# ScalarE's order in the prompt attention: exponentials of block i ahead of the copies of block i-1

## The reference, cut to what matters

```
s = (q_nope . k_nope + q_pe . k_pe) * SCALE      # 128 queries x (i+1)*128 keys
s = where(causal, s, -1e30)
pr = softmax(s)
out_block = pr @ v
```

## Time and profile before

| | |
|---|---|
| time, median of 3 runs | 2477.78 us (2474.61 to 2484.24) |
| the profiled execution's own time | 2484.98 us |
| its span | 2483.2 us |
| mean granted TensorE clock | 0.959 of full speed |
| busy share of the span | PE 93%, DVE 54%, ACT 25%, POOL 16% |
| the prompt attention's blocks | 1011 to 1315 us of the span, four pairs |

### The profile page before, as it was taken

The page is one execution under the profiler, slowest core; times in us unless marked ns, Lnnn a source line. Parts: engine busy times, 40 slices in busy tenths (PEclk is TensorE's granted clock), DMA queues, the critical chain, the costliest instruction groups (busy, mean ns, idle before and its releaser), DMA issues.

```text
span 2483.2 us, 36895 instructions
## 1 busy us (share of the span) xinstructions
PE 2314.1 (93%) x14466; PEld 2146.1 (86%) x14466; DVE 1351.2 (54%) x2071; ACT 632.7 (25%) x1043; POOL 388.6 (16%) x248
## 2 busy tenths in 40 slices
PE   6999999999998998788877879999999999999896
PEld 6999999999998997455444559999999999999896
DVE  6444444444446642887688973644444444444746
ACT  5211111111113241333332342311111111112523
POOL 0000000000000001999999100000000000000000
PEclk9999999999999999788879989999999999999998
DMA  4111111111111104000013511111111111111201
GB/s 142 49 45 42 42 42 51 34 51 51 51 51 34 51 26 51 14 14 13 0 47 102 163 54 37 51 52 51 42 43 50 37 48 50 35 51 51 67 27 70
DMA packets 53998, 123.01 MB, mean 50 GB/s; under 512 B 9985, under 2 KB 30882, under 8 KB 53730
## 3 DMA queue, kind: packets, MB, share of 16 engines
q1 hardware_dynamic: 47730, 112.92, 15.4%
q10 hardware_dynamic: 5264, 5.67, 0.8%
q0 software_dynamic: 928, 3.38, 0.4%
HBM read 115.85 MB, written 6.09 MB: 49 GB/s over the span
## 4 chain that ended last, share of the span: by engine, by line
PE 79%; DVE 11%; ACT 4%; issue 3%; DMA 1%; SPq 1%; ACTq 0%; DVEq 0%
PE ps L426 24%; PE ps L428 23%; PE ps L427 23%; PE ps L587 4%; DVE cacc L1593 2%; PE ps L612 1%; PE ps L602 1%; ACT pr L1047 1%; DVE cacc L1511 1%; DVE cacc L1509 1%; PE ps L744 1%; DMA raw<-in_wstream 1%; DVE rstd L1209 1%; DVE q L1527 1%; ACT sq L810 1%
## 5 line engine op out<-in xcount | busy, mean ns | idle before, releaser
L426 PE MATMUL ps<-n_hi,wlo 128*128 128x352 f32 x2832 | 924.6, 326 | 27.2 <-DVE wlo L1192 11.7
L428 PE MATMUL ps<-n_hi,whi 128*128 128x352 f32 x2832 | 914.4, 323 | 0.0
L427 PE MATMUL ps<-n_lo,whi 128*128 128x352 f32 x2832 | 913.1, 322 | 0.0
L426 PEld LDWEIGHTS ps<-n_hi,wlo 128*128 128x128 f32 x2832 | 535.5, 189 | 31.3 <-DVE wlo L1192 12.6
L427 PEld LDWEIGHTS ps<-n_lo,whi 128*128 128x128 f32 x2832 | 537.0, 190 | 2.1 <-issue 0.2
L428 PEld LDWEIGHTS ps<-n_hi,whi 128*128 128x128 f32 x2832 | 536.1, 189 | 0.0
L1257 DVE TENSOR_TENSOR gu<-ps,rstd 128x704 f32<-128x704 f32 x132 | 117.6, 891 | 506.8 <-PE ps L428 506.8
L426 PE MATMUL ps<-hid_hi,wlo 128*128 128x352 f32 x1104 | 360.9, 327 | 18.5 <-DVE h L1239 18.3
L428 PE MATMUL ps<-hid_hi,whi 128*128 128x352 f32 x1104 | 356.7, 323 | 0.0
L427 PE MATMUL ps<-hid_lo,whi 128*128 128x352 f32 x1104 | 356.2, 323 | 0.0
L1239 DVE SCALAR_TENSOR_TENSOR h<-ps,h 128x352 f32<-128x352 f32 x552 | 273.7, 520 | 150.4 <-PE ps L428 149.2
(11 more groups left out here) (181 smaller groups left out, 1854.4 us busy)
## 6 DMA issues: line engine op xcount, KB each, us to landing
raw<-in_wstream SPq DMA_DIRECT2D x167, 512.0 KB, 3.6
ctile<-in_cache SPq DMA_DIRECT2D x100, 144.0 KB, 2.4
ctile<-in_cache ACTq DMA_DIRECT2D x28, 144.0 KB, 2.7
pw<-in_pairw SPq DMA_DIRECT2D x4, 800.0 KB, 4.4
h<-in_xT SPq DMA_DIRECT2D x2, 1408.0 KB, 9.8
out_yT<-n POOLq DMA_DIRECT2D x2, 1408.0 KB, 6.2
h<-in_xT ACTq DMA_DIRECT2D x4, 352.0 KB, 5.4
out_ckvT<-ckv SPq DMA_DIRECT2D x1, 1056.0 KB, 9.1
```

The costliest lines, as they stand in the source:

```text
L426: nc.tensor.matmul(out, w_l, x_h, start=first, stop=False)
L427: nc.tensor.matmul(out, w_h, x_l, start=False, stop=False)
L428: return nc.tensor.matmul(out, w_h, x_h, start=False, stop=last)
```

## The change

In ScalarE's loop over the blocks, the copies of block i-1's transposed probabilities come after the two exponentials of block i instead of before them. Nothing else changes: the same instructions run, with the same waits on each of them.

```diff
             for i in range(QB):
-                if i:
-                    untile(i - 1)
                 for hh in range(2):
                     u = 2 * i + hh
                     act.wait_ge(s_max, 2 * QB * p + (u + 1))
                     w = (i + 1) * P
                     nc.scalar.activation(pr[:, i % 2, hh, 0:w], psf[:, 1024 * hh:1024 * hh + w], ACT.Exp,
                                          bias=stat[:, 4 + u % 4:5 + u % 4],
                                          accum_out=stat[:, 8 + u % 4:9 + u % 4]).then_inc(s_free, 1)
+                if i:
+                    untile(i - 1)
                 if i >= 2:
                     high_av(i - 2)
             untile(QB - 1)
```

## The result

The changed kernel takes 2466.86 us (median of 17 runs, 2449.91 to 2476.45), the kernel before 2480.86 in the same comparison (17 runs, 2472.31 to 2488.42). The ratio is 0.9938, 95% interval 0.9918 to 0.9958: 15 us by the ratio, 14.0 by the medians. That is clear of no change, but the interval (0.42% to 0.82%) holds the half per cent that the prediction took as its border. The prediction was 2464, with a range from 2453 to 2478.

The account below looks back on a forecast made before the run. TensorE, busy 93% of the span, bounds the kernel, except in prompt attention, where it waits for ScalarE's exponentials. Gains of 10.6 + 5.4 + 4.6, say 20 us, less 5.2 given back, net 14.8: rounded to 2464 us, range 2453 to 2478.

Parts of the forecast that it names:

- Direct early waits: Prompt attention, blocks 2 to 5: TensorE's waits before its scores go, 2.6 us a pair, 10.6 over four.
- The earlier clock: Early attention blocks: TensorE's clock rises sooner, some 13 us instead of 22 in pairs one and four; 5.4 us, bounds 0 and 9.
- Late blocks: Attention from block 4 on: two short TensorE holes become one; -4.6 us over four pairs, bounds +12 and -10.
- VectorE's delay: Attention normalisations slowed by GpSimd: 0.88 us a block, now standing in the late chain; above 1 us the prediction falls.
- The bound of +12: Late attention blocks, worst case: each loses as much as GpSimd's disturbance of VectorE, 1 us, together +12 us.
- Gross 20: Prompt attention, whole gain before any give-back: 10.6 + 5.4 + 4.6, say 20 us.
- Given back in the sample stage: Sample stage: 26 us more of GpSimd's taps run there, 3.1 iterations at 1.7 us more, 5.2 us lost.
- Behind it the shift arrives whole: After the sample stage: TensorE bounds everything again, so the remaining gain reaches the end undiminished, net 14.8 us.
- Early only with a late loss of 2: Attention: early waits go, clock rises when it did, late blocks lose 2 us; 2472 us (2466 to 2476), chance 0.25.
- The slower rival: Attention blocks 4 to 6: one 2 us hole pulls the clock down for long; 2488 us (2480 to 2496), chance 0.07.
- The better rival: Attention: normalisations mostly start before GpSimd's add, clock stays up from block 3; 2457 us (2451 to 2460), chance 0.12.

Follow-up runs that it names:

- early-only kernel: Kernel before with the new copy order in blocks 1 to 4 only, old order in blocks 5 to 7: 2467.04 us, ratio 0.9937.

## Why the prediction was right, point by point

**Direct early waits: 2.6 us a pair, 10.6 in all.** Right. S(1) to S(2) went from 3.11 to 2.67 (0.44, forecast 0.45) and S(3) to S(4), in a pair that was at low clock in both kernels, from 6.91 to 6.02 (0.89, forecast 0.61). S(2) to S(3) went from 5.21 to 4.39 (0.82, forecast 0.61). S(4) to S(5), in pairs at full clock there, went from 5.28 to between 4.2 and 4.8 (0.5 to 1.1, forecast 0.98). Together 2.7 to 3.3.

**The earlier clock: 5.4 us.** Right in kind, mis-sized by half. The early blocks gained 22.0 us in the first profiles (23.9 by the means of two each), of which 11 to 13 are direct by the sums above; 9 to 13 are left for the clock, at or above the upper bound of 9. This is got by subtraction, and no run shows it by itself. The first pair's low stretch ended 9.1 us after S(1) instead of 22, not 13 as I had put it, and the second pair's after 7.0, where I had booked nothing for that pair. A second profile of the kernel before has low stretches of 22 us in all four pairs, so there was more to win than in the one profile that I read. The Trainium skill's sentence that activity releases the throttle (TensorE: Matmul & The Clock Gate, What's actually happening) agrees with three of the pairs, whose low stretch ended earlier than before, 7.0 to 11.5 us after S(1). In the third it ended after 15.3 us (14.2 before), though TensorE was busy for 18.00 of the 18.16 us to S(5): the missing gaps did not set the moment alone.

**Late blocks: -4.6 us.** This is the step that failed. They cost +2.7 (131.8 to 134.5; means of two profiles 129.9 and 133.4, +3.5). The chain was the forecast one, and S(6) to S(7) came out at 8.65, 7.98, 8.52 and 9.82 us, 7.5 less than before in all (forecast 6.0 less). S(5) to S(6) cost 2.1 (forecast 1.6; the prediction's 7.85 for it should read 7.88, which changes nothing). What was under-priced is S(7) to V(7): 14.77, 15.80, 18.22 and 18.88, 8.1 more than before in all, where the forecast had 0.2 less. VectorE's delay was not it: over blocks 4 to 7 the normalisations took 0.86 us a block more than undisturbed ones, against the 0.88 forecast. What had no price is the clock. From S(7) to V(7) it was low for 0, 3.4, 6.8 and 6.8 us in the four pairs, before for 0, 3.4, 3.4 and 0, and the pairs with more of it are the longer ones. The bound of +12 held it. Without GpSimd's taps the same stretch took 14.2 us in every pair with no low clock; that GpSimd's delay is what brings the clock down there is likely, but not shown.

**Gross 20.** 19.3 in the first profiles, 20.4 by the means. That the sum came out is luck: the clock term was 4 to 8 us too low and the late term 7 to 8 too high, and the two errors cancel.

**Given back in the sample stage: 5.2 us.** 4.9 in the first profiles (127.5 to 132.4), 5.1 in the second ones (122.5 to 127.6). The size is right; the working is only partly borne out. The stage is shorter with GpSimd out of it (118.8 and 120.1) and longest where the attention ended earliest with GpSimd at work (139.2). But GpSimd ran 83.7 us into the early-only kernel's stage and 83.9 into the changed one's, and the stages took 122.8 and 132.4. So how long they run side by side does not set the loss alone. That it is how VectorE's and GpSimd's taps fall together fits the small taps (16.0 and 27.6 us), but no run changes that by itself.

**Behind it the shift arrives whole.** Neither shown nor refuted. Of the 17.7 us by which the changed kernel's first profile led at the 1100th matmul of the stage, 12.8 were left at the end, but 3.3 of the 17.7 stood before the first S(1), where both kernels do the same. In the second profiles 19.5 of 20.1 were left. Differences of this size come between executions; I made no experiment on it.

**The rivals.** Early only with a late loss of 2 described the late side better than the forecast did, but its clock term was too small. The slower rival's mechanism occurs: pairs 3 and 4 have 10.2 and 13.7 us at low clock in the late blocks. Before S(7) it is no cost of the change, for the old order has it just as much (13.7 in the third pair of before and in two pairs of the early-only kernel, most of it there). After S(7) it may be one: the four profiles with the new order in the late blocks and GpSimd at work have 17 to 24 us at low clock from S(7) to V(7), the five with the old order 0 to 12. The better rival's mechanism was in the early blocks, where a normalisation took 0.48 instead of 2.59. Its condition is harder to read than the prediction had it: the 2.59 one is itself recorded as starting 0.04 us before the add (1020.71 and 1020.75 in the earlier trace rows).

## What to carry to other kernels

When one engine serves two chains, look for the instruction that holds up each and interleave them by that; moving a whole group from one side to the other moves the wait with it. In blocks 5 to 7 two copies behind two exponentials gained nothing (ratio 1.0013), one copy behind each of them 0.9%. And price the clock with more than one profile: removing 11 to 13 us of gaps from blocks that ran mostly at 1.2 GHz gained 22 to 24 us, and a longer stretch at low clock took back what the chain should have gained late by its own durations.

## What the runs showed of the hardware

A VectorE instruction of 32 columns takes 0.24 us without GpSimd at work and 0.69 on the mean of 40 in the changed kernel's sample stage. Of these 40, 28 took 0.2 to 0.3 us, six some 2.35 and six some 1.10; each of the six long ones ended 0.05 us after an add of GpSimd that was under way when it began. The Trainium skill (SBUF — State Buffer, Who interferes with whom) says that a VectorE instruction with two inputs in that memory contends with a GpSimd one that reads it; the trace agrees, with 27.6 us for 40 instructions against 9.7. After a late gap TensorE's clock can stay low though the engine is then busy: in the third pair of before it was low from 1201.4 to 1211.7 us while TensorE was busy 9.9 of these 10.3, and in the first pair, after a gap of the same 1.46 us, for 3.4.
